# Routed experts of a decoder step: which operand stands in the gate and up products

## What is computed

```python
def swiglu(x, wg, wu, wd):
    return (jax.nn.silu(x @ wg) * (x @ wu)) @ wd

...
    def expert_block(args):
        xblk, e = args
        return swiglu(xblk, w_gate[e], w_up[e], w_down[e])

    yb = lax.map(expert_block, (xb, blk_e)).reshape(P, D)
    return jax.ops.segment_sum(yb * row_w[:, None], row_tok, num_segments=T)
```

## Time and profile before

| | us |
|---|---|
| median of 3 runs | 1863.98 |
| lowest and highest | 1863.68, 1868.23 |
| profiled execution: span | 1871.3 |
| stretch of the experts, first to last product of `experts` | 1044 to 1827 |

### The profile page before, as it was taken

The page is one execution under the profiler, slowest core; times in us unless marked ns, Lnnn a source line. Parts: engine busy times, 40 slices in busy tenths (PEclk is TensorE's granted clock), DMA queues, the critical chain, the costliest instruction groups (busy, mean ns, idle before and its releaser), DMA issues. The chain is left out here.

```text
span 1871.3 us, 24616 instructions
## 1 busy us (share of the span) xinstructions
PE 1777.9 (95%) x8684; PEld 1217.7 (65%) x8684; DVE 695.1 (37%) x1483; ACT 417.6 (22%) x843; POOL 349.0 (19%) x287
## 2 busy tenths in 40 slices
PE   7999999999999999999999989999999999999990
PEld 7999999999755557988764444444444444444440
DVE  3112433453455656654874222222222222222225
ACT  3112222322345554111100111111111111111114
POOL 0000330420200000000175112212222222222223
PEclk9999999999999999999999999999999999999995
DMA  6331633442312217442243799999999999999966
GB/s 214 98 103 55 188 111 107 156 118 101 113 44 57 71 55 291 151 147 68 94 194 104 238 367 378 384 379 375 368 373 369 369 367 364 362 365 365 344 175 216
DMA packets 133019, 411.61 MB, mean 220 GB/s; under 512 B 17620, under 2 KB 79092, under 8 KB 115332
## 3 DMA queue, kind: packets, MB, share of 16 engines
q1 hardware_dynamic: 108418, 319.77, 45.9%
q0 software_dynamic: 21504, 73.87, 15.2%
q10 hardware_dynamic: 3026, 17.04, 2.3%
HBM read 339.11 MB, written 73.96 MB: 221 GB/s over the span
## 5 line engine op out<-in xcount | busy, mean ns | idle before, releaser
L2446 PE MATMUL e_G<-wb,pages 128*128 128x512 f32 x1072 | 473.6, 595 | 6.4 <-DMA wb<-in_w_exp_gu 6.1
L2446 PEld LDWEIGHTS e_G<-wb,pages 128*128 128x128 f32 x1072 | 204.4, 191 | 264.4 <-issue 264.4
L2437 PE MATMUL e_Y<-mixT,e_aT 128*128 128x512 f32 x544 | 246.0, 595 | 3.7 <-ACT e_aT L2308 3.6
L2279 POOL DMA_INDIRECT d_base<-e_y_sb,e_s_idx x68 | 107.7, 1584 | 587.9 <-DMA d_base<-e_y_sb,e_s_idx 524.6
L2437 PEld LDWEIGHTS e_Y<-mixT,e_aT 128*128 128x128 f32 x544 | 98.0, 190 | 102.7 <-issue 102.1
L1291 PE MATMUL banks<-x_hi,gw_hi 128*128 128x352 f32 x464 | 151.6, 327 | 1.4 <-DVE r_srg L1083 1.4
L180 PE MATMUL banks<-w_hi,x_hi 128*128 128x244 f32 x512 | 142.9, 279 | 9.7 <-DVE x_lo L234 8.7
L1291 PE MATMUL banks<-x_hi,gw_lo 128*128 128x352 f32 x464 | 149.0, 321 | 0.0
L1291 PE MATMUL banks<-x_lo,gw_hi 128*128 128x352 f32 x464 | 148.9, 321 | 0.0
L180 PE MATMUL banks<-w_hi,x_lo 128*128 128x244 f32 x512 | 142.1, 277 | 0.0
L180 PE MATMUL banks<-w_lo,x_hi 128*128 128x244 f32 x512 | 141.7, 277 | 0.0
(11 more groups left out here) (388 smaller groups left out, 2683.7 us busy)
## 6 DMA issues: line engine op xcount, KB each, us to landing
wb<-in_w_exp_gu SPq DMA_DIRECT2D x64, 2048.0 KB, 12.9
mixT<-in_w_exp_dn SPq DMA_DIRECT2D x68, 1024.0 KB, 7.4
gw_sb<-in_w_gate SPq DMA_DIRECT2D x20, 512.0 KB, 6.7
d_proj<-o_sb SPq DMA_DIRECT2D x8, 1098.0 KB, 6.1
d_gateT<-r_g_out ACTq DMA_DIRECT2D x16, 528.0 KB, 2.6
pages<-in_cache_both SPq DMA_DIRECT2D x64, 128.0 KB, 2.0
wb<-in_w_exp_gu ACTq DMA_DIRECT2D x4, 2048.0 KB, 20.8
w_sb<-in_w_in SPq DMA_DIRECT2D x7, 976.0 KB, 11.1
```

The costliest lines, as they stand in the source:

```text
L2279: g.indirect_dma_start(base, bass.IndirectOffsetOnAxis(ap=s_idx[s][:, 0:1], axis=0), y_sb[:, c, :], None, compute_op=ALU.add).then_inc(y_o ...
L2437: mm = t_.matmul(Y[q][:], aT[:, c, k, :], w_d[:, s, k, q * 512:(q + 1) * 512], start=k == 0, stop=k == 1)
L2446: mm = t_.matmul(G[c], xT[:, c, k, :], w_gu[s][:, :, k, :], start=k == 0, stop=k == KD - 1)
```

## The change

`gate_up` (and its first call, in `trunk`) changes operands: for each u of four groups of 128 hidden units (two of gate, two of up) and each of the eight slices k, the weights stand and the 128 tokens of `xT` move. G then has a hidden unit in each partition. VectorE's second product writes straight into `aT`, with plain rows; `turn_act`, `turned_act`, the tiles `A` and `act_s` and two semaphores go, and `down` waits for `act_ok`. On the host the down weights are laid out so that hidden unit k*128 + p stands in partition p.

```diff
-                mm = t_.matmul(Y[0][:, 0, :], xT[:, 0, k, :], wb[0][:, :, k, :], start=k == 0, stop=k == KD - 1)
+            for u in range(4):
+                for k in range(KD):
+                    if u == 0 and k == 4:
+                        pe.wait_ge(xT_dve, 1)
+                    mm = t_.matmul(Y[0][:, 0, u * P:(u + 1) * P], wb[0][:, u // 2, k, (u % 2) * P:(u % 2 + 1) * P], xT[:, 0, k, :], start=k == 0, stop=k == KD - 1)
...
-            def turned_act(n, c):
-                act.wait_ge(a_turned, n)
-                s_.copy(aT[:, c].rearrange("p k n -> p (k n)"), A[:, 0:2 * P]).then_inc(aT_ok, 1)
...
-                v.tensor_tensor(act_s[:, c, :].rearrange("p (k q) -> p q k", k=2), sig[:, c, :].rearrange("p (q k) -> p q k", k=2),
-                                G[c][:, FF:2 * FF].rearrange("p (q k) -> p q k", k=2), ALU.mult).then_inc(act_ok, 1)
+                v.tensor_tensor(aT[:, c].rearrange("p k n -> p (k n)"), sig[:, c, :], G[c][:, FF:2 * FF], ALU.mult).then_inc(act_ok, 1)
...
             def down(n, c, s, n_in, n_free):
                 pe.wait_ge(d_in[s], n_in)
-                pe.wait_ge(aT_ok, n)
+                pe.wait_ge(act_ok, n)
...
-                    mm = t_.matmul(G[c], xT[:, c, k, :], w_gu[s][:, :, k, :], start=k == 0, stop=k == KD - 1)
+                for u in range(4):
+                    for k in range(KD):
+                        if u == 0 and k == 4:
+                            pe.wait_ge(xT_dve, n)
+                        mm = t_.matmul(G[c][:, u * P:(u + 1) * P], w_gu[s][:, u // 2, k, (u % 2) * P:(u % 2 + 1) * P], xT[:, c, k, :], start=k == 0, stop=k == KD - 1)
                 mm.then_inc(gu_done, 1)
-
-            def turn_act(n, c, n_free):
-                pe.wait_ge(act_ok, n)
-
-                pe.wait_ge(aT_ok, n_free)
-                for k in range(2):
-                    mm = t_.transpose(A[:, k * P:(k + 1) * P], act_s[:, c, k * P:(k + 1) * P], ident[:])
-                mm.then_inc(a_turned, 1)
...
-        "w_exp_dn": i["w_exp_down"].reshape(NE, P, 2 * D),
+        "w_exp_dn": i["w_exp_down"].reshape(NE, 2, P, D).transpose(0, 2, 1, 3).reshape(NE, P, 2 * D),
```

More of the change, by code:

```diff
@@ L2163, in _ @@
             pe.wait_ge(xT_act, 1)
-            for k in range(KD):
-                if k == 4:
-                    pe.wait_ge(xT_dve, 1)
-                mm = t_.matmul(Y[0][:, 0, :], xT[:, 0, k, :], wb[0][:, :, k, :], start=k == 0, stop=k == KD - 1)
+            for u in range(4):
[3 more added lines that the diff above has]
+                    mm = t_.matmul(Y[0][:, 0, u * P:(u + 1) * P], wb[0][:, u // 2, k, (u % 2) * P:(u % 2 + 1) * P], xT[:, 0, k, :], start=k == 0, stop=k == KD - 1)
             mm.then_inc(e_gu_done, 1)
@@ L2184, in experts @@
         sig = sb("sig", [P, 2, FF])
-        act_s = sb("act_s", [P, 2, FF])
         aT = sb("aT", [P, 2, 2, P])
@@ L2189, in experts @@
         G = [GX[0][:, i, :] for i in range(2)]
-        A = ctx.enter_context(nc.psum_tensor("e_A", [P, 512], F32))
         Y = [ctx.enter_context(nc.psum_tensor(f"e_Y{i}", [P, 512], F32)) for i in range(2)]
         (over_in, over_ok, over_clear, s_ok, y_out, sig_ok, a1_ok,
-         act_ok, a_turned, aT_ok, d_done, y_act, y_dve) = [sem(n) for n in
+         act_ok, d_done, y_act, y_dve) = [sem(n) for n in
             "over_in over_ok over_clear s_ok y_out sig_ok a1_ok "
-            "act_ok a_turned aT_ok d_done y_act y_dve".split()]
+            "act_ok d_done y_act y_dve".split()]
         block = ctx.enter_context(nc.Block())
@@ L2324, in _ @@
                     gate(s, (s - 1) % 2)
-                if s >= 2:
-                    turned_act(s - 1, s % 2)
                 if s >= 1:
@@ L2335, in _ @@
                     gate(at(act, r, W, s), 1 - c)
-                    turned_act(at(act, r, W, s - 1), c)
                     turned(at(act, r, 2 * W, 2 * s + 1), c)
@@ L2340, in _ @@
             gate(at(act, r, W, 0), 1)
-            turned_act(at(act, r, W, -1), 0)
             weigh(at(act, r, W, -1), 0, 2, at(act, r, 16 * W, -48))
-            turned_act(at(act, r, W, 0), 1)
             weigh(at(act, r, W, 0), 1, 3, at(act, r, 16 * W, -32))
@@ L2442, in gate_up @@
                 pe.wait_ge(xT_act, n)
-                for k in range(KD):
-                    if k == 4:
-                        pe.wait_ge(xT_dve, n)
-                    mm = t_.matmul(G[c], xT[:, c, k, :], w_gu[s][:, :, k, :], start=k == 0, stop=k == KD - 1)
-                mm.then_inc(gu_done, 1)
-            def turn_act(n, c, n_free):
-                pe.wait_ge(act_ok, n)
-                pe.wait_ge(aT_ok, n_free)
-                for k in range(2):
-                    mm = t_.transpose(A[:, k * P:(k + 1) * P], act_s[:, c, k * P:(k + 1) * P], ident[:])
-                mm.then_inc(a_turned, 1)
+                for u in range(4):
[3 more added lines that the diff above has]
+                        mm = t_.matmul(G[c][:, u * P:(u + 1) * P], w_gu[s][:, u // 2, k, (u % 2) * P:(u % 2 + 1) * P], xT[:, c, k, :], start=k == 0, stop=k == KD - 1)
+                mm.then_inc(gu_done, 1)
             for s in range(W):
@@ L2463, in _ @@
                     gate_up(s + 1, s % 2, s, 16)
-                if s >= 1:
-                    turn_act(s, (s - 1) % 2, s - 1)
             more = quads(pe)
@@ L2472, in _ @@
                     gate_up(at(pe, r, W, s + 1), c, s, now)
-                    turn_act(at(pe, r, W, s), 1 - c, at(pe, r, W, s - 1))
             r = pe.snap(more + NE // W)
             down(at(pe, r, W, -1), 0, 2, at(pe, r, 16, 0), at(pe, r, W, -2))
-            turn_act(at(pe, r, W, 0), 1, at(pe, r, W, -1))
             down(at(pe, r, W, 0), 1, 3, at(pe, r, 16, 0), at(pe, r, W, -1))
```

## The result

| | before | changed |
|---|---|---|
| median of 12 runs each, us | 1865.7 | 1867.9 |
| lowest to highest | 1862.7 to 1869.9 | 1865.2 to 1875.9 |
| profiled execution: time, span | span 1871.3 | 1872.2, 1870.3 |

A forecast was written before the change was run, and what follows sets the result against it. TensorE was taken to bound the kernel, with GpSimd's additions close behind. Blocks +2.9, first block +0.3, stall -1.8 and end -1.1 gave +0.3 us on 1863.98: 1864.3 us, range 1856 to 1873.

The forecast's parts named there:

- The pace: In the experts' stage TensorE sets the pace, 11.40 us a block, with GpSimd's additions to HBM close behind.
- The distance of the passes: In gate and up, 128-column passes come 0.1115 us apart, so 64 take 7.14 us for 6.87 a block.
- the rival of the long run: In gate and up, 64 pairs in a row cannot beat 0.113 us each: 1871 us, slower by 0.4%; chance 0.14.
- The rival with the turns' 0.109: Gate and up passes come at 0.109 us like the tokens' turns: 1854 to 1855 us, faster by 0.5%; chance 0.12.
- that of a load that is not hidden: In gate and up, load and stream follow one another, 0.215 us a pass: +427 us, 2290 us; chance 0.02.
- The loop's code stays: In the experts' loop, no code is fetched again; the rival with fetches in 16 turns: +98 us, 1962 us, chance 0.02.
- The prediction's 109.2 ns: The skill's distance of warm matmuls at 128 columns, for gate and up; by it the sum would be 9 us lower.
- The lower bound: For gate and up passes, no load for much less than 0.108 us, the distance in rows with 64 moving columns.
- The block: In the experts' stage, gate and up 0.27 us more, transposes 0.22 less: +0.046 us a block, +2.9 us over 64.
- the last but one down product: At the end, it need not wait for transposes and copy, starting at 1816.95 and not 1818.03: -1.1 us.
- the stall at 1783 us: TensorE's one steady-part stall, 1.83 us behind late additions, would go as TensorE arrives later without a copy: -1.8 us.
- The base: The difference against the profiled span of 1871.3 us, 7.3 us above the median, is carried over to the median 1863.98 us.

The follow-up runs named there:

- experiment 6: The kernel before with the turn of the activations and its copy left out, long passes kept: ratio 0.9931, -12.9 us.
- Experiments 3 and 4: The changed kernel with 96, then 64, of 128 token columns moving in the loop's gate and up: ratio 1.0001; 1890.3 us (single execution, another chip).
- experiment 7: The changed kernel with TensorE's value load of the number of further blocks moved from the loop's entry to the front of its program: ratio 1.0020.
- experiment 8: The changed kernel with SyncE issuing the fifth block's gate and up weights ahead of the lists of the further blocks: ratio 1.0008.

## Why the prediction was right, and where it was off

- **The pace.** That TensorE's own path sets it was right: transposes put back cost 9 us, left out they give 13. That a cheaper block would run into the additions was right too (experiment 6, 5.4 us of stalls from 1150 to 1750 us).
- **The distance of the passes** was the term on which all hung, and it came out as taken: 0.1117 us against 0.1115. Sixty-four in a row run like sixteen, so the rival of the long run (0.113) fell. The rival with the turns' 0.109 and that of a load that is not hidden (0.215) fell with the same row. The loop's code stays: the page has 45 packets on the instruction queue q8 for 42, in 16 turns of the loop. The prediction's 109.2 ns was an estimate, for two cycles a column, from a formula of the Trainium skill (TensorE: Matmul & The Clock Gate, Back-to-back issue gap). The section gives that formula for a matmul by itself and says that it counts too little at few columns, where each matmul has a load; the prediction did not say so. The trace has 111.7 ns at 128 columns, 2.5 more, while at 512 and 256 columns the same estimate, 429.2 and 215.8 ns, agrees with the 429 and 216 of the traces.
- **The lower bound was wrong.** I took 0.108 from the router as the least a load can cost. Experiments 3 and 4 give 0.1112 and 0.1107. At 128 columns the distance is within 1% of the 0.1107 us with 64.
- **The block** was right: +0.046 predicted, 11.45 for 11.41 us measured as means over more than fifty blocks. So was the last but one down product, which follows gate and up at once.
- **The step that failed** is the stall at 1783 us, counted as -1.8. I argued that TensorE would get there later and find the weighing done. In the changed kernel's profile it found three stalls, 2.8 us of idle time and nearly 2 more of a lowered clock; with the value load moved (experiment 7) there is one, of 1.84 us, and with the first refill earlier (experiment 8) there are two, of 1.63 and 1.19. The additions had slowed down again, and the down product waits for their weighing whether or not the activations need a copy. Without this credit the sum would have been +2.1 us; the measured +3.9 has 2.1 in its interval (2.0 to 5.6), and 0.3 lies outside it.
- **The base.** The sum starts from the span of one execution and is carried over to the median. That execution was unlike the others: its span of 1871.3 us lies above the time of every one of the 12 runs of the kernel before (at most 1869.9). Its stall need not stand in the runs whose median was forecast. The median of 3 runs, 1863.98, was also 1.7 us under that of 12.
- **A cost left out** is the 1.2 us at the loop's entry, which with the 2.1 above would make 3.3. I had excluded a fetch of code, rightly, and not thought of the value load, which leaves no idle time in any profile with longer passes. Where a wait for `wb` follows, as before, it may cost nothing. This cost, the credit and the base all make the forecast low: 1864.3 for the measured median of 1867.9. It holds because together they stay small against its range, not because they cancel.

## What to carry to other kernels

Moving a transpose out by letting the other operand stand has a price when the passes get short: before writing it, compare what the transpose costs with what the new weight loads cost. In the float32 passes of this kernel, 128 columns do not quite cover a load and 256 do; here sixteen long passes turned into sixty-four short ones gave back 0.28 us a block for the 0.22 of the turn. When a chain of transfers stands right behind the bound, a stall in one profile is neither a cost nor a credit: it moves from run to run, and only the repeated rows of the steady part can be summed.

## What the runs showed that was not expected

- A float32 pass of TensorE with its own load of 128 x 128 takes 0.1107, 0.1112 and 0.1117 us with 64, 96 and 128 moving columns, and 0.216 with 256. At 128 columns it is the same whichever operand stands (7.14 and 7.15 us for 64).
- A value load that left no idle time behind 16 long passes leaves 0.8 to 1.2 us behind 64 short ones, in six of eight profiles; in the two with SyncE's first refill issued earlier it leaves none. The cause stays open.
- TensorE's loss need not come out in full where a second chain stands close behind: +0.28 us in each of 64 blocks, 18 us, cost 15.3 (12.1 to 18.5, so perhaps all of it); a further 0.22, 14 us, cost 9.3 (5.0 to 13.6), with stalls that vanished from the end of the profile.
